# A seventh place for the next expert's first weight unit, copied into the ring by GpSimd

## Chip, cores and metric

One core of a Trainium2 chip runs the whole program. The metric is the device time of one execution in microseconds; the number given for a kernel is the median of its runs.

## What is computed

One layer of a decoder for 256 prompt tokens and 8 x 8 sample tokens, D = 1024, all in float32: modulated RMSNorm, differential attention with a paged cache beside an mLSTM branch, their merge, and then a mixture of experts, which is what the change is about:

```python
logits = (xt @ p['w_router']) + p['b_router']
topv, topi = lax.top_k(logits, TOP_K)             # 4 of 32 experts for each of 320 tokens
...
gu = xb @ p['w_gu'][e] + p['b_gu'][e]             # 1024 -> 2 x 1024
gate = jnp.minimum(gu[:, :D_FF], SWIGLU_LIMIT)
up = jnp.clip(gu[:, D_FF:], -SWIGLU_LIMIT, SWIGLU_LIMIT)
act = (up + 1.0) * gate * jax.nn.sigmoid(SWIGLU_ALPHA * gate)
return (act @ p['w_down'][e] + p['b_down'][e]) * w[:, None]   # 1024 -> 1024, summed over the 4
```

An expert's weights are 12 MB, so the 32 experts read 384 MB; the four gate/up units of an expert hold a quarter of the input rows each, the two down units half of them each.

## The kernel before

The kernel has one hand-written instruction stream for each engine, tied together by semaphores. Everything up to the router is straight-line code. The expert stage is a loop over *blocks*: an expert's tokens are taken 32 at a time (SLOTS), and an expert has one to ten blocks, by how many tokens chose it. With this input there are 55 blocks for 32 experts. The tables with the experts' block counts are made on the chip (`ints`, read back with `value_load` after the semaphore `tables`).

All large weights go through `ring`, six places of 2 MB (`[P, 6, 4096]` float32, 16 KB a partition each). `moe_slot[i]` is the place of an expert's unit i: units 0 to 3 are the gate/up quarters, 4 and 5 the down halves. SP issues the loads in that order, for one expert after another (`expert_weights`, L2217 issues): ahead of unit i of expert e it waits until TensorE has read unit i in all blocks before e (`unit_read[i]`, L2209). `unit_landed` tells of a landing.

TensorE's block (`expert_block`, L1015) runs, in this order: the bias rows; quarter 0; the transposes of the previous block's activations (L989); quarter 1; the previous block's down projection with units 4 and 5; the gather of the next block's tokens; quarter 2; half of the previous block's sums (`combine`); quarter 3; transposes of the gathered rows (L967), the other half of the sums, and transposes of the token weights (L1012). Each quarter waits for its unit's landing (`gate_up_quarter`). Unit 0 of an expert is thus free 2 us into its last block, and units 4 and 5 only in the next expert's first block. Nearly all these matmuls are recorded under L513, the helper `mm`.

VectorE makes the selection tiles of the next gather (L1658, needed by `gather`) and the weighted ones (L1664), adds the sums (L1686) and does the clamps and products of the activation. ScalarE copies from PSUM. GpSimd issues loads and stores before the stage, has nothing to do within it, and stores the outputs at the end.

`hT`, the normalized and transposed tokens, is last read by the router's matmuls and the transposes of `h2`, before the stage.

## Time and profile before

| | |
|---|---|
| time, median of 3 runs | 1680.15 us (1673.82 to 1682.11) |
| profiled execution | 1677.65 us, of which the span is 1675.4 us |
| granted TensorE clock, mean | 0.91 of full speed |
| busy: TensorE, VectorE, ScalarE, GpSimd | 86%, 36%, 16%, 4% |
| DMA | 505.69 MB, mean 302 GB/s |
| expert stage | about 613 to 1642 us of the span |

In the profile PE is TensorE's matmuls and PEld its weight loads, DVE is VectorE, ACT ScalarE, POOL GpSimd and SP the engine that only issues. A q behind the name means the engine's sequencer. The span is the time from the first to the last instruction of the profiled execution; the two microseconds beside it lie around the program. In the timeline, an entry in square brackets gives the idle time ahead of an instruction and what ended it: `<-DMA ring<-in_w_gu` is a wait for a gate/up unit to land. In the stretches table, each row has the stretch, its length, the busy time of PE, PEld, DVE, ACT and POOL (with instructions), the granted share of TensorE's clock, the busy share of the DMA engines and GB/s. A row of the list of waits ends in: us in total, times, longest us. In the views by line, a landing is counted from the issue of the load.

### The profile page before, as it was taken

Reading aid. Unit: us, or ns where it says so; the run is one execution under the profiler, and the core shown is the slowest. Engines: PE = TensorE matmul, PEld = TensorE weight load, DVE = VectorE, ACT = ScalarE, POOL = GpSimd, SP = SyncE. Lnnn points to the kernel's source line nnn. Section 1 sums busy time; section 2 is a strip of 40 time slices with the busy share of each in tenths; the row PEclk is TensorE's granted clock in tenths of the full one; section 3 lists DMA queues with packets and bytes.
Section 4 is the critical chain, followed back from the end, with each engine's and each line's share of the span. In section 5 each row is a group of like instructions: output and inputs, shape, how many; then the busy total and the mean of one; then the engine's idle time right before and its main releaser. Section 6 shows DMA issues by size and latency. Waiting matters only on the chain.

```text
span 1675.4 us, 40558 instructions
## 1 busy us (share of the span) xinstructions
PE 1438.3 (86%) x16467; PEld 804.7 (48%) x16468; DVE 595.4 (36%) x1317; ACT 275.1 (16%) x641; POOL 61.4 (4%) x114
## 2 busy tenths in 40 slices
PE   5798899989999789997999797977959877798794
PEld 3345665557766445553555354533525443344452
DVE  2325553714544333432433233222322423132324
ACT  2004441321210121111111011100101111010111
POOL 2002220000010000000000000000000000000000
PEclk9799998978999979998999899987969988798997
DMA  9525896670057229969999999999999969997850
GB/s 332 193 77 182 294 381 248 211 253 1 1 151 302 101 111 404 388 258 419 404 396 383 424 417 409 426 418 424 401 419 417 408 285 388 417 401 297 369 232 32
DMA packets 80702, 505.69 MB, mean 302 GB/s; under 512 B 6575, under 2 KB 6695, under 8 KB 47666
## 3 DMA queue, kind: packets, MB, share of 16 engines
q1 hardware_dynamic: 72642, 479.86, 71.2%
q0 software_dynamic: 8016, 25.24, 4.6%
q8 instruction: 27, 0.44, 0.1%
q14 instruction: 17, 0.14, 0.0%
HBM read 499.97 MB, written 5.11 MB: 301 GB/s over the span
## 4 chain that ended last, share of the span: by engine, by line
PE 69%; DMA 20%; DVE 6%; issue 2%; ACT 1%; SPq 1%; DVEq 0%; POOL 0%; ACTq 0%; POOLq 0%
PE psum L513 62%; DMA ring<-in_w_gu 15%; DMA ring<-in_w_down 4%; PE psum L672 2%; PE psum L1012 1%; PE psum L967 1%; PE psum L989 1%; DMA ring<-in_w_ada 1%; DVE region L1285 1%; SPq L2217 1%; PE psum L704 0%; ACT region L1773 0%; DVE hT L1171 0%; DVE region L1252 0%; SPq L2222 0%
## 5 line engine op out<-in xcount | busy, mean ns | idle before, releaser
L513 PE MATMUL psum<-ring,region 128*32 128x256 f32 (+1 forms) x11072 | 665.0, 390 | 122.3 <-DMA ring<-in_w_gu 120.2
L513 PEld LDWEIGHTS psum<-ring,region 128*32 128x32 f32 x11072 | 347.6, 114 | 393.7 <-DMA ring<-in_w_gu 131.1
L1686 DVE TENSOR_TENSOR region<-region,psum 128x1280 f32<-128x1280 f32 x110 | 163.2, 1483 | 568.2 <-PE psum L513 568.2
L1773 ACT ACTIVATE region<-psum 128x256 f32<-128x256 f32 (+6 forms) x391 | 164.3, 422 | 1148.8 <-PE psum L513 503.8
L513 PE MATMUL psum<-region 32*128 32x320 f32 (+10 forms) x2652 | 247.2, 421 | 9.4 <-ACT region L1773 3.4
L513 PEld LDWEIGHTS psum<-region 128*32 128x32 f32 (+5 forms) x2652 | 106.3, 139 | 111.2 <-issue 74.5
L513 PE MATMUL psum<-hT,ring 128*128 128x320 f32 x448 | 124.5, 436 | 0.0
L513 PEld LDWEIGHTS psum<-hT,ring 128*128 128x128 f32 x448 | 84.5, 191 | 35.4 <-issue 1.9
L513 PE MATMUL psum<-ring,hT 128*128 128x512 f32 (+1 forms) x192 | 86.4, 607 | 6.1 <-DVE hT L1177 6.1
L1664 DVE TENSOR_SCALAR region<-region 128x128 f32<-128x128 f32 x165 | 47.3, 343 | 98.5 <-issue 98.5
L513 PEld LDWEIGHTS psum<-ring,hT 128*128 128x128 f32 (+1 forms) x192 | 33.1, 177 | 55.0 <-issue 48.7
L672 PE MATMUL psum<-keep,ring 128*128 128x128 f32 x256 | 40.3, 294 | 8.7 <-ACT region L1773 4.4
L513 PE MATMUL psum<-region,ring 128*128 128x320 f32 (+1 forms) x192 | 45.7, 386 | 1.4 <-DVE region L1545 1.4
L2165 POOL DMA_DIRECT2D out_y_prompt<-region x2 | 1.1, 536 | 1126.2 <-DVE region L1764 1126.2
L513 PEld LDWEIGHTS psum<-region,ring 128*128 128x128 f32 x192 | 33.5, 201 | 12.9 <-issue 2.8
L513 PE MATMUL psum<-oT,bias_hot 96*32 96x256 bf16 x440 | 22.1, 276 | 18.8 <-issue 17.5
L672 PEld LDWEIGHTS psum<-keep,ring 128*128 128x128 f32 x256 | 28.9, 147 | 18.7 <-DVE region L1285 10.1
L498 POOL DMA_DIRECT2D ring<-in_cache_v x64 | 34.4, 537 | 76.3 <-issue 76.3
L513 PE MATMUL psum<-region,keep 128*128 128x320 f32 (+7 forms) x90 | 31.5, 481 | 5.2 <-ACT region L2009 3.3
L513 PE MATMUL psum<-ring,cT 128*32 128x512 f32 x192 | 29.7, 768 | 6.8 <-DMA ring<-in_w_ada 6.8
L1012 PE MATMUL psum<-keep,region 128*128 128x128 f32 x165 | 35.2, 291 | 0.0
L1703 DVE TENSOR_SCALAR region<-psum 128x256 f32<-128x256 f32 x55 | 23.3, 424 | 32.4 <-PE psum L513 32.4
(301 smaller groups left out, 886.3 us busy)
## 6 DMA issues: line engine op xcount, KB each, us to landing
ring<-in_w_gu SPq DMA_DIRECT2D x128, 2048.0 KB, 12.2
ring<-in_w_down SPq DMA_DIRECT2D x64, 2048.0 KB, 10.9
ring<-in_w_ada SPq DMA_DIRECT2D x12, 2048.0 KB, 14.5
ring<-in_w_in SPq DMA_DIRECT2D x11, 2048.0 KB, 19.9
ring<-in_cache_k SPq DMA_DIRECT2D x64, 256.0 KB, 5.4
ring<-in_cache_v POOLq DMA_DIRECT2D x64, 256.0 KB, 5.5
ring<-in_w_out SPq DMA_DIRECT2D x2, 2048.0 KB, 22.0
ring<-in_w_up_a SPq DMA_DIRECT2D x1, 2048.0 KB, 10.7
```

Of the source, the lines that this page charges most:

```text
L498: engine.dma_start(dst[:, g, :], cache[bass.ds(page, 1), :, :].rearrange("o p c -> p (o c)"))\
L513: return pe.matmul(out, lhsT, rhs, start=start, stop=stop, skip_group_check=True)
L672: last = pe.transpose(out[:, P * h:P * h + P], kc[:, g, P * h:P * h + P], ident)
L967: last = pe.transpose(psum[:, B_HG, P * j:P * j + P], rows[:, j, :], ident)
L989: last = pe.transpose(psum[:, B_Y, P * j:P * j + P], rows[:, j, :], ident)
L1012: last = pe.transpose(psum[:, B_Y, t0:t0 + m], selw[0:m, j, :], ident[0:m, 0:m])
L1285: dve.tensor_copy(kTb[:, :, PAGE * g:PAGE * g + PAGE], bank("kTb", b, g).rearrange("p (h k) -> p h k", h=H))\
L1664: last = dve.tensor_scalar(selw[:, j, :], lanes, pos[:, j, column], wts[:, j, expert], ALU.is_equal, ALU.mult)
L1686: dve.tensor_tensor(acc_pairs[:, r], acc_pairs[:, r], psum[:, B_SUM:B_SUM + GROUPS, 0:NT], ALU.add)\
L1703: dve.tensor_scalar(act_g, psum[:, B_GATE, 0:WIDE], LIMIT, None, ALU.min).then_inc(gate_clamped, 1)
L1773: return act.activation(out, src, ACT.Copy)
L2217: sp.dma_start(dst, src).then_inc(unit_landed[moe_slot[i]], 16)
```

## The change

The kernel gets one more place of 2 MB, `landing`. It costs no memory: `hT` becomes the tail of `region`, and `landing` covers it and the 1536 columns ahead of it, which held squares that are no longer needed by then. Unit 0 of experts 1 to 31 is loaded there and not into the ring. SP issues that load (`fill_landing`) right behind unit 5 of the expert before, after a wait until that expert's own unit 0 has left the place; the one for expert 1 goes out when the transposes of `h2` are done. GpSimd, in a loop of its own, waits until the ring's place is free and the landing place filled, and copies 128x4096 float32 over in four pieces, each of which raises `first_moved`. TensorE's quarter 0 waits for four pieces in place of the landing. For expert 0, whose unit 0 is loaded as before, four memsets of one word raise the semaphore. SP's loop ends one expert earlier, and the last expert is issued behind it.

```diff
--- before.py
+++ after.py
@@ -135,7 +135,6 @@
 
         ring = sb("ring", [P, RING, UNIT])
         xT = sb("xT", [P, KT, NT])
-        hT = sb("hT", [P, KT, NT])
         keep = sb("keep", [P, n_keep])
         vecT = sb("vecT", [P, 128])
         bias_hot = sb("bias_hot", [P, SLOTS], BF16)
@@ -146,7 +145,8 @@
         small = sb("small", [P, 64])
         oT = sb("oT", [P, H, NT])
         hmT = sb("hmT", [P, H, NT])
-        region = sb("region", [P, REGION])
+        region = sb("region", [P, REGION + KT * NT])
+        hT = region[:, REGION:REGION + KT * NT].rearrange("p (k t) -> p k t", k=KT)
         ints = sb("ints", [1, N_INTS], I32)
         psum = ctx.enter_context(nc.psum_tensor("psum", [P, 8, 512], F32))
 
@@ -288,6 +288,7 @@
         fin_rstd = E.take(3)
         fin_gain = E.take(D)
         x1_sq = Area(REGION - KT * NT).take(KT, NT)
+        landing = region[:, REGION + KT * NT - UNIT:REGION + KT * NT]
         assert E.at <= REGION - KT * NT
         pos = E.take(3, ROUNDS * NE)
         y_out = h2_tok
@@ -302,6 +303,7 @@
         LAM, NLAM, COEF, GS = small[:, 0:4], small[:, 4:5], small[:, 5:6], small[:, 6:7]
         MX, LS, RC = small[:, 8:12], small[:, 12:16], small[:, 16:20]
         M0 = small[0:H, 20:29]
+        pool_word = small[0:1, 40:44]
         BG = small[0:H, 29:31]
         SC = small[:, 32:40]
 
@@ -368,6 +370,8 @@
         blocks_ready = sem("blocks_ready")
         begun_ready = sem("begun_ready")
         bias_in = sem("bias_in")
+        landing_filled = sem("landing_filled")
+        first_moved = sem("first_moved")
         tables = sem("tables")
         mean_inverse = sem("mean_inverse")
         mean_root = sem("mean_root")
@@ -974,7 +978,10 @@
 
             def gate_up_quarter(c, expert):
 
-                pe.wait_ge(unit_landed[moe_slot[c]], 16 * expert + (landed_base[c] + 16))
+                if c == 0:
+                    pe.wait_ge(first_moved, 4 * expert + 4)
+                else:
+                    pe.wait_ge(unit_landed[moe_slot[c]], 16 * expert + (landed_base[c] + 16))
                 u = ring[:, moe_slot[c], :].rearrange("p (j f) -> p j f", j=2)
                 for j in range(2):
                     for q, out_bank in ((0, B_GATE), (1, B_UP)):
@@ -2158,6 +2165,22 @@
             pool.dma_start(bd_rows[0:NE, :], I["b_down"]).then_inc(moe_in, 16)
             pool.dma_start(fin_gain, I["g_final"].to_broadcast([P, D])).then_inc(gain_in, 16)
 
+            first_unit = ring[:, moe_slot[0], :]
+            pool.wait_ge(unit_landed[moe_slot[0]], landed_base[0] + 16)
+            for piece in range(4):
+                pool.memset(pool_word[:, piece:piece + 1], 0.0).then_inc(first_moved, 1)
+            pool.wait_ge(tables, 1)
+            with pool.Fori(1, NE) as e:
+                before = pool.value_load(ints[0:1, bass.ds(e + (AT_BLOCKS - 1), 1)], min_val=1,
+                                         max_val=MAX_BLOCKS)
+                pool.wait_ge(unit_read[0], before)
+                filled = nc.snap(16 * e, [mybir.EngineType.Pool])
+                pool.wait_ge(unit_landed[moe_slot[0]], landed_base[0] + 16)
+                pool.wait_ge(landing_filled, filled)
+                for piece in range(4):
+                    part = slice(UNIT // 4 * piece, UNIT // 4 * piece + UNIT // 4)
+                    pool.tensor_copy(first_unit[:, part], landing[:, part]).then_inc(first_moved, 1)
+
             for j, (t0, n) in enumerate(TILES):
                 for half in range(2):
                     pool.wait_ge(*drained("y", j, half))
@@ -2200,10 +2223,16 @@
             gu = I["w_gu"].rearrange("e (c p j) f -> e c p (j f)", c=4, j=2)
             dn = I["w_down"].rearrange("e (h c p j) f -> e h p c (j f)", h=2, c=2, j=2)
 
+            def fill_landing(expert):
+
+                sp.dma_start(landing, gu[expert, 0].rearrange("o p f -> p (o f)")).then_inc(landing_filled, 16)
+
             def expert_weights(expert, blocks_before):
                 for i in range(RING):
                     if blocks_before is None:
                         sp.wait_ge(*last_use[units[len(units) - RING + i][0]])
+                    elif i == 0:
+                        continue
                     else:
 
                         sp.wait_ge(unit_read[i], blocks_before)
@@ -2217,11 +2246,17 @@
                     sp.dma_start(dst, src).then_inc(unit_landed[moe_slot[i]], 16)
 
             expert_weights(slice(0, 1), None)
+            sp.wait_ge(*full("h2", 2, 1))
+            fill_landing(slice(1, 2))
             sp.wait_ge(tables, 1)
-            with sp.Fori(1, NE) as e:
+            with sp.Fori(1, NE - 1) as e:
                 before = sp.value_load(ints[0:1, bass.ds(e + (AT_BLOCKS - 1), 1)], min_val=1,
                                        max_val=MAX_BLOCKS)
                 expert_weights(bass.ds(e, 1), before)
+                sp.wait_ge(first_moved, 4 * e + 4)
+                fill_landing(bass.ds(e + 1, 1))
+            expert_weights(slice(NE - 1, NE), sp.value_load(
+                ints[0:1, AT_BLOCKS + NE - 2:AT_BLOCKS + NE - 1], min_val=1, max_val=MAX_BLOCKS))
 
 
 _OUTS = [
```

## Rows read from the trace of the kernel before

**Rows 1.** page, part 4: chain that ended last, by engine; first the span
```profile
span 1675.4 us, 40558 instructions
...
PE 69%; DMA 20%; DVE 6%; issue 2%; ACT 1%; SPq 1%; DVEq 0%; POOL 0%; ACTq 0%; POOLq 0%
```

**Rows 2.** stretches table of the expert stage, then its list of waits
```profile
613.00:1642.00 1029.00, 888.61 (x13506) 462.01 (x13505) 318.22 (x707) 125.95 (x330) 0.00 (x0) 0.92 0.91 379
...
PE psum L513 <- DMA ring<-in_w_gu: 120.2, 32, 10.8
```

**Rows 3.** timeline of TensorE, one block: start us, us, what, xcount, [idle before]
```profile
644.67 0.40 PE L513 MATMUL psum<-oT,bias_hot 96*32 96x256 bf16 x8 [0.43 <-issue]
...
644.88 1.92 PE L513 MATMUL psum<-ring,region 128*32 128x256 f32 x32
...
647.16 5.39 PE L513 MATMUL psum<-ring,region 128*32 128x256 f32 x96
...
660.59 0.40 PE L513 MATMUL psum<-oT,bias_hot 96*32 96x256 bf16 x8 [0.37 <-issue]
```

**Rows 4.** timeline of TensorE, a stalled block
```profile
764.12 3.64 PE L513 MATMUL psum<-ring,region 128*32 128x256 f32 x32 [7.61 <-DMA ring<-in_w_gu]
769.02 7.18 PE L513 MATMUL psum<-ring,region 128*32 128x256 f32 x96 [0.63 <-DMA ring<-in_w_gu]
```

**Rows 5.** timeline of TensorE, from three other stalled blocks
```profile
957.20 5.39 PE L513 MATMUL psum<-ring,region 128*32 128x256 f32 x96 [0.62 <-DMA ring<-in_w_gu]
...
966.99 1.93 PE L513 MATMUL psum<-ring,region 128*32 128x256 f32 x32 [0.35 <-DMA ring<-in_w_gu]
...
1351.82 5.39 PE L513 MATMUL psum<-ring,region 128*32 128x256 f32 x96 [1.25 <-DMA ring<-in_w_gu]
...
1590.87 3.64 PE L513 MATMUL psum<-ring,region 128*32 128x256 f32 x32 [7.49 <-DMA ring<-in_w_gu]
```

**Rows 6.** timeline, expert 1, first block; then the chain (start us, us)
```profile
624.78 1.93 PE L513 MATMUL psum<-ring,region 128*32 128x256 f32 x32 [0.30 <-DMA ring<-in_w_gu]
...
629.68 6.88 PE L513 MATMUL psum<-ring,region 128*32 128x256 f32 x96 [2.54 <-DMA ring<-in_w_gu]
...
617.55 12.09 DMA ring<-in_w_gu
```

**Rows 7.** stretches table, the block of rows 4
```profile
756.12:784.24 28.12, 19.52 (x249) 9.10 (x249) 5.86 (x15) 2.26 (x7) 0.00 (x0) 0.76 1.01 428
```

**Rows 8.** timeline of SP's queue: issues of the weight units
```profile
746.53 2.10 SPq L2217 DMA_DIRECT2D ring<-in_w_down  x2
749.76 4.74 SPq L2217 DMA_DIRECT2D ring<-in_w_gu  x4
```

**Rows 9.** issues at 726.6 and 728.9, 746.5, 1235.5, 1327.2, 1432.2 us: to landing
```profile
DMA to landing us min/median/max: 7.4/8.7/10.1
...
DMA to landing us min/median/max: 7.7/7.7/7.7
...
DMA to landing us min/median/max: 9.0/9.0/9.0
...
DMA to landing us min/median/max: 9.8/9.8/9.8
...
DMA to landing us min/median/max: 10.8/10.8/10.8
```

**Rows 10.** VectorE by shape: xcount | busy us, mean ns | idle before
```profile
L1686 DVE TENSOR_TENSOR region<-region,psum 128x1280 f32<-128x1280 f32 x108 | 160.2, 1483 | 561.8 <-PE psum L513 561.8
...
L1658 DVE TENSOR_SCALAR region<-region 128x32 f32<-128x32 f32 x162 | 28.4, 235 | 0.0
L1710 DVE TENSOR_TENSOR region<-region 128x256 f32<-128x256 f32 x55 | 23.4, 425 | 17.2 <-ACT region L2060 17.2
```

**Rows 11.** timeline of VectorE in the block of rows 3
```profile
647.75 0.86 DVE L1664 TENSOR_SCALAR region<-region 128x128 f32<-128x128 f32 x3 [1.73 <-issue]
648.52 0.53 DVE L1658 TENSOR_SCALAR region<-region 128x32 f32<-128x32 f32 x3
```

## The prediction

> **What bounds the kernel now.** I read the page first. The chain that ended last is 69% TensorE and 20% DMA, so neither alone is the bound [rows 1]. The stretches table then puts the expert stage at 1029 of 1675.4 us, with the DMA engines 0.91 busy and TensorE granted 0.92 of its clock; the list of waits says that TensorE stood 120.2 us for gate/up weights, in 32 waits [rows 2]. That is the most an earlier weight unit could give back.
>
> The timeline shows where those waits lie. There are 55 blocks. A block that waits for nothing takes 15.9 us, from 644.67 to 660.59: biases, quarter 0 at 644.88, quarter 1 and the block before's down projection (5.39 us) from 647.16, the gather at about 652.5, quarters 2 and 3 [rows 3]. An expert's six units arrive 4.9 us apart when the queue is full, 29 us together. So an expert of two or three blocks leaves time to load the next, an expert of one block (13 of 32, by the release times) does not, and the expert behind it waits. In all but the first of those cases it looks like this: quarter 0 waits 7.6 us and starts as its unit lands, at 764.12; quarter 1 starts at 769.02, as the second unit lands, 4.9 us later [rows 4]. Twelve blocks have this form, in the last one quarter 0 starts at 1590.87 [rows 5]. Two details matter. Quarter 0 takes 3.64 us there against 1.93 us elsewhere: the granted clock of that stretch is 0.76, so part of it, this quarter included, ran at the lower level of 1.2 GHz after the idle wait [rows 3, 4, 5, 7]. And the idle time ahead of quarter 1 is then 0.63 us, no more [rows 4]. The second unit, not the first, holds the block, but by 0.6 to 1.25 us only [rows 4, 5]; I take 0.7.
>
> **What the seventh place gains.** It lets the next expert's first unit be asked for as soon as the present expert's six are, not when the ring's first unit was read for the last time. But behind a one-block expert that was already so: its two down units were issued at 746.53, and the next expert's first unit followed at 749.76, held by SP's own order [rows 8]. Its landing was 14.3 us after issue, all of it queueing behind the down units. There the new place changes nothing: the transfer waits for the same bytes, 12 times in 12.
>
> Behind an expert of several blocks the first unit does come earlier, and no one waits for it there. What it leaves is a queue shorter by one unit (4.9 us) in that expert's last block. The next five units still wait for TensorE's reads. Where DMA had been idle, an issue lands after 7.4 to 7.7 us; the first down unit of the ten one-block experts that follow a longer one took 7.7 to 9.8 us [rows 9], and only what is above 7.7 can be won, 0 to 2.1 us each, 11 us if all of it goes. What took that excess is not plain (some of it appears with the earlier unit just landing, which the change does not remove), so I take 5 us, bounds 0 and 11. One gain is surer: expert 1. Its first unit now loads in the idle queue before the stage, so its second, issued at 617.55, no longer queues: 7.4 us instead of 12.1, landing at 625.0. Quarter 1 then follows quarter 0 and the transposes, at about 627 instead of 629.68 [rows 6, 9]: 2.5 us.
>
> **What the copy costs.** Each of experts 1 to 31 adds four GpSimd copies of 128x1024 float32, and TensorE's wait for all four before quarter 0. The trace has no copy on GpSimd, so I bound it by VectorE: 425 ns for 256 columns and 1483 ns for 1280 [rows 10] are 1.03 ns a column and 0.16 us fixed, so 1.22 us a piece, 4.9 us for four, and 0.1 us to see the semaphore: **5.0 us**. The low end is half of that, 2.5 us, and the high end twice, 9.9 us; nothing in the trace puts it nearer either, so I take the VectorE figure. The Trainium skill pulls both ways here: "GPSIMD Engine Reference", 4.1 Engine selection, calls one-input elementwise work on this engine roughly line-rate, while "Trainium Architecture — The Big Picture", The five engines, in one table, has streaming elementwise work two times slower than on VectorE. No run shown so far decides between them; by the first page the sum would be the forecast's, by the second that of the slow-copy rival.
>
> Behind a longer expert the copy is hidden: the ring's first unit is read 2.2 us into the last block, the copy ends at 7.3, and quarter 0 of the next block comes at 16.1 [rows 3]. If the copy took over 13 us that cover would be gone. In the twelve stalled blocks it is bare. The landed unit is what TensorE waits for, so quarter 0 starts 5.0 us later; it and the transposes take 4.3 us at the lower clock, and quarter 1, which had 0.7 us to spare, starts 5.0 - 0.7 = 4.3 us late. Everything behind it in the block is TensorE's own work, and the block ends 4.3 us late. Six of the twelve have quarter 3 waiting 0.35 us for its unit as well, as at 966.99, which takes 0.35 us off each [rows 5].
>
> Does the delay last? The next transfers are released by TensorE's reads, so the schedule behind moves with it. Only where the expert is again a single block does the queue have some slack: its first down unit took 9.0 us at 1235.5 and 10.8 us at 1432.2, against 7.7 us unqueued [rows 9], so 1.3 and 3.1 us of those two delays are absorbed before the next wait.
>
> The other edits cost nothing that I can see. The fill's new wait on the copies stands in SP's queue behind the sixth unit's issue, ahead of the next expert's second unit; TensorE needed those copies for quarter 0 of the same block, so it is over long before. The fill for expert 1 waits for the transposes of h2, when SP has nothing else to issue. GpSimd is idle from its last load to the final stores, so its loop, its register load and its four small memsets delay nobody. Folding hT into the region moves addresses and no instruction.
>
> **The sum.** 12 x 4.3 = 51.6; less 6 x 0.35 = 2.1; less 1.3 + 3.1 = 4.4; less 2.5 for expert 1; less 5 for the shorter queue: **+37.6 us**. The profiled execution took 1677.65 us, of which the span is 1675.4, so 1715 for its like. It lies 2.5 us under the median of the runs (1680.15), which makes the forecast 1717.8, said as 1718 us; the times below are on the median's footing too.
>
> With the copy at 2.5 us the delay is 1.8 us: 21.6 - 2.1 - 3.1 - 7.5 = +8.9, or 1689. At 7 us, 6.3 each: 75.6 - 14.0 = +61.6, or 1742. At 9.9 us, 9.2 each: 110.4 - 14.0 = +96.4, or 1777.
>
> **The rivals.** (a) *The copy is slow*, near twice VectorE's time. For it speaks that the trace's GpSimd does nothing but issue DMAs, so nothing vouches for its rate. 1742 to 1777 us. (b) *VectorE and GpSimd get in each other's way.* In a longer expert's last block the copy stands from 2.3 to 7.3 us, as worked out above. VectorE's selection tiles are made from 3.1 to 4.4 us into a block, and the gather needs them at 7.9 [rows 3, 11]. If they had to wait for the last piece they would be ready at 7.3 + 1.3 = 8.6, 0.7 us late, in 18 experts: +13 on top, 1731. Against it: there are gaps between four pieces. The Trainium skill, "SBUF — State Buffer", Who interferes with whom, states such a lock: a port pair shared by the two, held for a whole instruction, which `tensor_scalar` can ask for in its fast mode. (c) *A fast copy*, 2.5 to 4 us: 1689 to 1707. (d) *The other side, faster:* the copy is so short that quarter 0 still ends before the second unit lands. That needs 0.7 us in all or less, 0.2 us a piece, shorter than a 128x32 operation of VectorE (235 ns [rows 10]); then only the gains are left, 2.5 + 11 = 13.5 us, 1667 us. It turns from gain to loss at a copy of about 1.8 us, if all 11 us come. (e) *The place doesn't do what it says*: the fill is never earlier where the stage stalls. That is already in the sum; with the 5 us gone as well it gives 1723.
>
> **How the numbers follow.** Forecast, a copy of 4 to 6 us without (b): 0.50 (with (e) in it). (a) 0.20, (b) 0.10, (c) 0.13, a copy of 1 to 2.5 us, which is no change that could be told: 0.05, (d) 0.02. About 0.5%, 8.4 us, is what a measurement of this kernel can tell from no change. Faster 0.02, same 0.05, slower 0.93. The range 1692 to 1765 leaves out the lower end of (c) and what is under it, and the upper end of (a), some 0.2 together.
>
> **What would show it.** In the new profile: four GpSimd copies of about 1.2 us for each expert, 124 in all; in the twelve stalled blocks a TensorE idle time of 12.5 to 16 us ahead of quarter 0, released by GpSimd and no longer by the DMA, and none ahead of quarter 1; unstalled blocks still at 15.9 us; quarter 1 of expert 1 near 627. Blocks of 16.6 us with the gather waiting for VectorE would mean (b). The forecast is wrong if the copy's time is another (12 us of result for each 1 us of copy), if quarter 0 runs at the full clock behind the longer wait (1.7 us less for each stall), or if the stalls themselves come earlier, which would mean that the fill overtakes something that I hold to be in its way.

## The result, and the profile after

| | before | after |
|---|---|---|
| time, median of 16 runs each | 1679.29 us | 1691.84 us (1682.42 to 1699.36) |
| ratio | 1 | 1.0098, 95% interval 1.0076 to 1.012 |
| profiled execution | 1677.65 us | 1692.39 us |
| span | 1675.4 us | 1690.8 us |
| first block's biases to the last block's | 613.5 to 1625.4: 1011.9 us | 612.7 to 1641.0: 1028.4 us |

The change makes the kernel 1.0% slower, 16 us by the ratio; the two medians stand 12.6 us apart. The forecast had the direction, and put the loss at 38 us. The measured time lies just under the range of 1692 to 1765.

The page of the changed kernel (span, the chain by engine, and GpSimd's group), which answers to rows 1:

```profile
span 1690.8 us, 41005 instructions
...
PE 74%; DMA 13%; DVE 6%; issue 3%; POOL 2%; ACT 1%; SPq 0%; POOLq 0%; DVEq 0%; ACTq 0%
...
L2182 POOL COPY ring<-region 128x1024 f32<-128x1024 f32 x124 | 123.7, 1041 | 943.8 <-DMA region<-in_w_gu 760.0
```

GpSimd copies 124 times, at 1041 ns a piece. Of the 31 groups of four, 27 were released by the landing of the unit and 4 by TensorE's last read of the ring's place. The chain has less DMA (13% for 20%) and more TensorE. The stretches table and the list of waits for the expert stage, against rows 2:

```profile
613.00:1658.00 1045.00, 874.89 (x13501) 459.23 (x13493) 326.32 (x707) 126.07 (x330) 123.68 (x124) 0.92 0.91 371
...
PE psum L517 <- POOL ring L2182: 148.9, 12, 14.4
```

The 120.2 us for gate/up weights are gone, and 148.9 us for GpSimd's copy stand in their place. It is 12 waits and not 32, as every stalled block now waits once only, ahead of quarter 0. The stalled block of rows 4 and the unstalled one behind it, in the timeline of all engines:

```profile
750.72 0.40 PE L517 MATMUL psum<-oT,bias_hot 96*32 96x256 bf16 x8 [0.38 <-issue]
...
758.70 3.99 POOL L2182 COPY ring<-region 128x1024 f32<-128x1024 f32 x4 [33.34 <-DMA region<-in_w_gu]
...
762.74 3.64 PE L517 MATMUL psum<-ring,region 128*32 128x256 f32 x32 [11.62 <-POOL ring L2182]
...
766.94 6.12 PE L517 MATMUL psum<-ring,region 128*32 128x256 f32 x96
...
781.10 0.40 PE L517 MATMUL psum<-oT,bias_hot 96*32 96x256 bf16 x8 [0.37 <-issue]
...
789.60 3.99 POOL L2182 COPY ring<-region 128x1024 f32<-128x1024 f32 x4 [26.91 <-DMA region<-in_w_gu]
...
797.02 0.40 PE L517 MATMUL psum<-oT,bias_hot 96*32 96x256 bf16 x8 [0.37 <-issue]
```

The first unit lands, and GpSimd starts at 758.70. Quarter 0 starts at 762.74, which is 4.04 us behind the start of the copy and 4.17 us behind the landing; in the kernel before it started 0.04 us behind the landing. It ran without pause into quarter 1, which came 4.20 us behind it, where rows 4 have 4.90 us with a pause of 0.63. Quarter 1 and the down projection together took less time than in rows 4 (6.12 us for 7.18). The unstalled block takes 15.92 us as before, and the copy in it is released by the landing, 8.5 us into the block; I had put it at 2.3. Another of the twelve, the first block of rows 5:

```profile
952.35 3.64 PE L517 MATMUL psum<-ring,region 128*32 128x256 f32 x32 [11.62 <-POOL ring L2182]
...
956.42 5.39 PE L517 MATMUL psum<-ring,region 128*32 128x256 f32 x96
```

Expert 1, against rows 6 (the first row is the start of the stage):

```profile
612.66 0.40 PE L517 MATMUL psum<-oT,bias_hot 96*32 96x256 bf16 x8 [0.47 <-ACT region L1780]
...
623.41 1.92 PE L517 MATMUL psum<-ring,region 128*32 128x256 f32 x32
...
625.69 5.39 PE L517 MATMUL psum<-ring,region 128*32 128x256 f32 x96
...
639.22 0.40 PE L517 MATMUL psum<-oT,bias_hot 96*32 96x256 bf16 x8 [0.31 <-issue]
```

Quarter 1 starts at 625.69 for 629.68, and the block takes 16.0 us for 20.6. SP's queue behind the one-block expert of rows 8, and the landing of that fill:

```profile
741.14 2.11 SPq L2246 DMA_DIRECT2D ring<-in_w_down  x2
743.53 0.42 SPq L2228 DMA_DIRECT2D region<-in_w_gu  x1
...
DMA to landing us min/median/max: 15.0/15.0/15.0
```

The fill comes out 2.4 us behind the first down unit, where rows 8 have 3.2, and lands 15.0 us later for 14.3: no gain in the stalls, as forecast. VectorE's two operations that GpSimd could have stood in the way of (rows 10 have the second at 235 ns, and the first took 343 ns before):

```profile
L1671 DVE TENSOR_SCALAR region<-region 128x128 f32<-128x128 f32 x162 | 51.2, 373 | 93.7 <-issue 93.7
L1665 DVE TENSOR_SCALAR region<-region 128x32 f32<-128x32 f32 x162 | 30.9, 250 | 0.0
```

As means they are 30 and 15 ns longer, 7.3 us of busy time over the whole stage. The mean hides what happens: nearly all take as long as before, and in three blocks, where the copy starts 2.5 us into the block, they go in step with its pieces. Rows 11 have 0.86 and 0.53 us for the same two groups:

```profile
721.37 3.99 POOL L2182 COPY ring<-region 128x1024 f32<-128x1024 f32 x4 [36.08 <-PE psum L517]
...
721.99 2.47 DVE L1671 TENSOR_SCALAR region<-region 128x128 f32<-128x128 f32 x3 [1.70 <-issue]
724.37 1.31 DVE L1665 TENSOR_SCALAR region<-region 128x32 f32<-128x32 f32 x3
```

That is what rival (b) describes. The tiles are ready 6.8 us into the block, and the gather starts at 7.7, so these blocks are no longer (15.9 us), and no unstalled block is.

### The profile page after: what moved, and what is told of

Same layout as the page of the kernel before. It is cut to its first block, busy times and chain, and to the rows that moved or that the text cites. A ratio compares the mean times of both kernels' runs of the same rounds, so it can differ in the third digit from the quotient of the medians.

```text
span 1690.8 us, 41005 instructions
## 1 busy us (share of the span) xinstructions
PE 1421.1 (84%) x16467; PEld 800.1 (47%) x16468; DVE 603.2 (36%) x1317; ACT 275.5 (16%) x641; POOL 185.3 (11%) x243
## 4 chain that ended last, share of the span: by engine, by line
PE 74%; DMA 13%; DVE 6%; issue 3%; POOL 2%; ACT 1%; SPq 0%; POOLq 0%; DVEq 0%; ACTq 0%
PE psum L517 67%; DMA region<-in_w_gu 11%; POOL ring L2182 2%; PE psum L676 2%; PE psum L996 1%; PE psum L1019 1%; PE psum L971 1%; DMA ring<-in_w_ada 1%; DVE region L1292 1%; DMA ring<-in_w_gu 1%; PE psum L708 0%; ACT region L1780 0%; DVE region L1178 0%; DVE region L1259 0%; SPq L2246 0%
## 5 line engine op out<-in xcount | busy, mean ns | idle before, releaser
L517 PE MATMUL psum<-ring,region 128*32 128x256 f32 (+2 forms) x11264 | 740.0, 390 | 156.5 <-POOL ring L2182 148.9
L517 PEld LDWEIGHTS psum<-ring,region 128*32 128x32 f32 (+1 forms) x11264 | 378.2, 113 | 465.8 <-POOL ring L2182 152.2
L517 PE MATMUL psum<-region 128*32 128x256 f32 (+11 forms) x2700 | 258.4, 423 | 18.3 <-DVE region L1184 9.0
L2182 POOL COPY ring<-region 128x1024 f32<-128x1024 f32 x124 | 123.7, 1041 | 943.8 <-DMA region<-in_w_gu 760.0
L517 PE MATMUL psum<-region,ring 128*128 128x320 f32 (+1 forms) x640 | 170.1, 421 | 1.4 <-DVE region L1552 1.4
L517 PEld LDWEIGHTS psum<-region,ring 128*128 128x128 f32 x640 | 117.9, 194 | 48.4 <-issue 4.9
L1671 DVE TENSOR_SCALAR region<-region 128x128 f32<-128x128 f32 x165 | 52.1, 373 | 98.5 <-issue 98.5
L1019 PEld LDWEIGHTS psum<-keep,region 128*128 128x128 f32 x165 | 18.5, 139 | 32.9 <-issue 32.9
L1665 DVE TENSOR_SCALAR region<-region 128x32 f32<-128x32 f32 x168 | 31.9, 250 | 0.0
L996 PEld LDWEIGHTS psum<-keep,region 128*128 128x128 f32 x110 | 17.2, 206 | 26.9 <-issue 25.7
L1717 DVE TENSOR_TENSOR region<-region 128x256 f32<-128x256 f32 x55 | 23.4, 426 | 17.0 <-ACT region L2067 16.8
## 6 DMA issues: line engine op xcount, KB each, us to landing
region<-in_w_gu SPq DMA_DIRECT2D x31, 2048.0 KB, 15.5
ring<-in_w_out SPq DMA_DIRECT2D x2, 2048.0 KB, 20.6
```

The costliest lines, as they stand in the source:

```text
L517: return pe.matmul(out, lhsT, rhs, start=start, stop=stop, skip_group_check=True)
L996: last = pe.transpose(psum[:, B_Y, P * j:P * j + P], rows[:, j, :], ident)
L1019: last = pe.transpose(psum[:, B_Y, t0:t0 + m], selw[0:m, j, :], ident[0:m, 0:m])
L1665: last = dve.tensor_scalar(sel[:, j, :], lanes[:, 0:SLOTS], pos[:, j, column], None, ALU.is_equal)
L1671: last = dve.tensor_scalar(selw[:, j, :], lanes, pos[:, j, column], wts[:, j, expert], ALU.is_equal, ALU.mult)
L1717: dve.tensor_tensor(act_g, act_g, act_s, ALU.mult).then_inc(gs_ready, 1)
```

## The sum, term by term

The same times can be read in each of the twelve stalled blocks of both profiles: from the block's start to the landing, from there to quarter 0, from there to quarter 1, from there to the next block's start, and the block after. Their sums over the twelve, after less before:

| term | forecast | measured |
|---|---|---|
| landing to quarter 0, for the copy, 12 times | 60.0 (5.0 us) | 49.5 (4.17 us for 0.04) |
| quarter 0 to quarter 1 | -8.4 | -10.6 |
| quarter 1 to the block's end | -2.1 | -9.3 |
| landing of the first unit, from the block's start | -9.4 (queue 5.0, slack 4.4) | -6.8 |
| expert 1 | -2.5 | -4.6 |
| other blocks (five took 16.2 to 16.3 us before) | 0 | -1.8 |
| sum | +37.6 | +16.4 |

Two things carry the difference of 21 us: the copy held quarter 0 for 0.9 us less each time (10.5), and the blocks were quicker from quarter 0 on by more than I had counted (2.2 to quarter 1, 7.2 behind it). The second is a matter of the clock. Six of the twelve quarters 0 rose to full speed within the quarter and took 3.23 to 3.62 us for 3.64; in three blocks of the kernel before this happened too, but quarter 1 then waited for its own unit and could not follow sooner. The stretches table for the first three parts of rows 4's stalled block in the kernel before (stretch, length, busy PE, PEld, DVE, ACT, POOL, granted clock, DMA share, GB/s):

```profile
764.12:769.02 4.90, 4.27 (x34) 1.71 (x35) 0.00 (x0) 0.38 (x1) 0.00 (x0) 0.50 1.00 428
769.02:772.70 3.68, 3.68 (x36) 1.77 (x40) 0.00 (x0) 0.00 (x0) 0.00 (x0) 0.50 1.00 427
772.70:776.00 3.30, 3.30 (x64) 1.80 (x60) 0.00 (x0) 0.00 (x0) 0.00 (x0) 1.00 1.05 447
```

and the like in the changed kernel:

```profile
762.74:766.94 4.20, 4.20 (x35) 1.69 (x35) 0.00 (x0) 0.00 (x0) 0.00 (x0) 0.50 0.99 421
766.94:768.30 1.36, 1.36 (x17) 0.66 (x20) 0.00 (x0) 0.38 (x1) 0.00 (x0) 0.50 1.02 434
768.30:773.00 4.70, 4.70 (x92) 2.63 (x88) 0.00 (x0) 0.00 (x0) 0.00 (x0) 0.98 0.95 373
```

In both TensorE had been idle for 8 to 12 us, and restarts at 0.50 of the clock, its 1.2 GHz level. Before, it pauses 0.63 us ahead of 769.02 and stays there for 8.6 us in all. After, it does not pause and is at full speed about 5.7 us behind quarter 0's start. Before, five of the other stalled blocks did the same, while six were back at full speed by quarter 1: 13.4 us from quarter 1 to the block's end, against 15.2 to 15.5. After, all twelve lie between 13.4 and 14.3. The quick ones end at 13.4 us with the wait of 0.35 us ahead of quarter 3 (before) and without it (after), so the 2.1 us forecast for these waits came to nothing, and all of the 9.3 us are the clock's.

## The experiments

All ratios are against runs of the kernel before on the same chip in the same session. "Stage" is the time from the first block's biases to the last's.

| run | ratio to before (95%) | stage, us | quarter 1 to block's end, twelve blocks |
|---|---|---|---|
| before | 1 | 1011.9 | six at 13.4, six at 15.2 to 15.5 |
| e5_before_again | one run, 1666 us | 1009.2 | seven at 13.4, five at 15.2 to 15.6 |
| after | 1.0098 (1.0076 to 1.012) | 1028.4 | 13.4 to 14.3 |
| e8_after_again | 1.0099 (1.0077 to 1.012) | 1027.9 | 13.4 to 14.1 |
| e1_no_copy | 0.9889 (0.9849 to 0.993) | 999.0 | 13.4 to 14.1 |
| e2_piece_waits | 0.9926 (0.9904 to 0.9948) | 1005.3 | 13.4 to 14.1 |
| e3_late_fill | 1.0118 (1.0084 to 1.0152) | 1031.4 | 13.4 to 13.9 |
| e4_copy_twice | 1.048 (1.0438 to 1.0521) | 1086.3 | 13.4 to 14.2 |
| e6_no_pause | 1.0244 (1.0219 to 1.0269) | 1051.7 | 13.4 to 14.1 |
| e7_half_us_delay | 0.995 (0.993 to 0.9971) | 1003.5 | 13.4 to 14.2 |
| e9_pause_filled | 1.0006 (0.9981 to 1.0031) | 1012.6 | 13.4 to 14.0 |
| e10_one_copy | one run, 1687 us | 1028.6 | 13.4 to 14.1 |

### e1_no_copy: the seventh place with a copy of no cost

```diff
-                    pool.tensor_copy(first_unit[:, part], landing[:, part]).then_inc(first_moved, 1)
+                    pool.memset(pool_word[:, piece:piece + 1], 0.0).then_inc(first_moved, 1)
```

> GpSimd's four copies are replaced by four memsets of one word, so nothing moves from the landing place into the ring (TensorE reads the ring's old unit 0 for every expert: that part of the result is left out). What is left is the seventh place with a copy of no cost. My theory: the copy is the whole of the loss, and the early place itself gives a little: 4.6 us at expert 1 and some us from a shorter queue, so 5 to 14 us faster than the kernel before, 1665 to 1674. Rival 1: the seventh place itself costs (the extra wait in SP's queue, the transfers in another order): at or above the kernel before, 1679 or more. Rival 2: the seventh place is worth as much as was meant, a 4.9 us unit for each of 13 stalls: about 50 us faster, 1630.

The kernel leaves out the move of the data, and so part of the result. 1657.87 us, 0.9889 of the kernel before: 18.6 us faster, 12 to 25 by the interval; 5 to 14 had been expected. Rivals 1 and 2 fall. Taken with the changed kernel's 1.0098 the copy costs 2.1%, 35 us. The timeline of the second of the stalled blocks:

```profile
943.59 3.60 PE L517 MATMUL psum<-ring,region 128*32 128x256 f32 x32 [9.12 <-POOL small L2182]
...
948.17 5.39 PE L517 MATMUL psum<-ring,region 128*32 128x256 f32 x96 [0.54 <-DMA ring<-in_w_gu]
```

The memsets still delay quarter 0 by 0.3 us. All twelve blocks are quick from quarter 1 on. In the stage's 12.9 us less than before, 10.6 come from there; that part is no merit of the seventh place, as e7 will show.

### e4_copy_twice: the copy doubled

```diff
+                copied = nc.snap(4 * e, [mybir.EngineType.Pool])
                 for piece in range(4):
                     part = slice(UNIT // 4 * piece, UNIT // 4 * piece + UNIT // 4)
+                    pool.tensor_copy(first_unit[:, part], landing[:, part]).then_inc(copied_once, 1)
+                pool.memset(pool_word[:, 0:1], 0.0)
+                pool.wait_ge(unit_landed[moe_slot[0]], landed_base[0] + 16)
+                pool.wait_ge(copied_once, copied)
+                for piece in range(4):
+                    part = slice(UNIT // 4 * piece, UNIT // 4 * piece + UNIT // 4)
                     pool.tensor_copy(first_unit[:, part], landing[:, part]).then_inc(first_moved, 1)
```

> The changed kernel with the four copies made twice over, the second time after a wait for the first; only the second time tells TensorE. A copy of 4.0 us becomes one of about 8.2. My theory: a stalled block pays all of it, 12 x 4.2 = 50 us, less 3 to 7 us that the queue's slack absorbs behind one-block experts: 43 to 48 us above the changed kernel, 1735 to 1740. Rival (the loss is from the wait's place or from VectorE standing behind GpSimd in the other blocks): other than in proportion to the stalls; with VectorE behind it, unstalled blocks longer than 15.9 us and over 60 us in all.

1.048 of the kernel before, 3.8% or 64 us above the changed kernel, and 58 us in the stage: more than the 43 to 48 us expected. The twelve stalled blocks pay 41.7 us of it ahead of quarter 0: the second copy holds it 4.1 us longer, 49.5 us in all, less 7.8 us as the units land earlier from the block's start. That is in proportion to the stalls. The rest, 16 us, is in other blocks, nearly all of it in three that did not stall before. GpSimd's and then TensorE's timeline, a block whose expert follows one of two blocks:

```profile
651.14 3.99 POOL L2184 COPY ring<-region 128x1024 f32<-128x1024 f32 x4 [26.82 <-DMA region<-in_w_gu]
...
655.26 4.40 POOL L2190 COPY ring<-region 128x1024 f32<-128x1024 f32 x4
...
656.12 0.40 PE L518 MATMUL psum<-oT,bias_hot 96*32 96x256 bf16 x8 [0.36 <-issue]
659.72 3.43 PE L518 MATMUL psum<-ring,region 128*32 128x256 f32 x32 [3.19 <-POOL ring L2190]
```

The fill had landed at 651.1, 18 us behind its issue, and not early in the last block; 8.5 us of copies reach 3.3 us past the point where quarter 0 wants them. So the cover that I gave the copy ("over 13 us") was 5.2 us here, and 7.6 us in the unstalled block of the changed kernel above. The changed kernel's 4.0 us fit in it; a copy of 9.9 us would not have.

### e3_late_fill: the early place made useless

```diff
-            fill_landing(slice(1, 2))
             sp.wait_ge(tables, 1)
+            sp.wait_ge(unit_read[0], sp.value_load(ints[0:1, AT_BLOCKS:AT_BLOCKS + 1], min_val=1,
+                                                   max_val=MAX_BLOCKS))
+            fill_landing(slice(1, 2))
...
                 sp.wait_ge(first_moved, 4 * e + 4)
+                after_this = sp.value_load(ints[0:1, bass.ds(e + AT_BLOCKS, 1)], min_val=1,
+                                           max_val=MAX_BLOCKS)
+                sp.wait_ge(unit_read[0], after_this)
                 fill_landing(bass.ds(e + 1, 1))
```

> The changed kernel, but the landing place is filled no earlier than the ring's first place was before: SP waits for TensorE's last read of unit 0 ahead of each fill, for expert 1 too. The copy is as it was. It is the changed kernel with its seventh place made useless. My theory: expert 1's gain of 4.6 us is lost and the 4 to 6 us from the shorter queue, so 8 to 11 us above the changed kernel, 1700 to 1703. Rival (the early place is worth nothing): 1692. Rival (it is worth what was meant): far above, 1740.

1.0118, against 1.0098 and 1.0099 for the changed kernel: 3 us above, and the intervals overlap. 8 to 11 us had been expected. The trace says where the difference lies. Expert 1's first block:

```profile
620.95 0.40 PE L517 MATMUL psum<-oT,bias_hot 96*32 96x256 bf16 x8 [0.76 <-DVE bias_hot L1677]
626.14 3.64 PE L517 MATMUL psum<-ring,region 128*32 128x256 f32 x32 [4.79 <-POOL ring L2182]
...
630.15 5.39 PE L517 MATMUL psum<-ring,region 128*32 128x256 f32 x96
...
643.67 0.40 PE L517 MATMUL psum<-oT,bias_hot 96*32 96x256 bf16 x8 [0.46 <-issue]
```

It takes 22.7 us for 16.0: 6.7 us lost, since the copy is now bare there too. The rest of the stage is 3.6 us shorter than in the changed kernel, and not longer. So in these profiles the early place is worth something at expert 1 alone. The 5 us that I gave the shorter queue are not seen.

### e2_piece_waits: TensorE waits piece by piece

```diff
-                if c == 0:
-                    pe.wait_ge(first_moved, 4 * expert + 4)
-                else:
+                if c:
                     pe.wait_ge(unit_landed[moe_slot[c]], 16 * expert + (landed_base[c] + 16))
...
                     for q, out_bank in ((0, B_GATE), (1, B_UP)):
+                        if c == 0:
+                            pe.wait_ge(first_moved, 4 * expert + (2 * j + q + 1))
```

> The changed kernel, but TensorE's quarter 0 waits for one piece ahead of each fourth of its matmuls (a piece of 1024 columns is just what one fourth reads) and not for all four ahead of the first. Copies of 1.0 us and fourths of 0.9 us (at the lower clock) then overlap, and quarter 1 comes 0.7 us late in a stalled block and no longer 3.1 us. My theory: 12 x 2.4 = 29 us less than the changed kernel's 1692, or 1663; if the short waits between the fourths keep the granted clock low for longer, up to 9 us of that are lost: 1672. Either way faster than the kernel before (1679). Rival (it is not the bare copy that costs, but what lies around it): unchanged, 1692.

1662.78 us, 0.9926 of the kernel before (0.9904 to 0.9948): the lowest ratio of the versions with all of the work in them, though e7's interval overlaps it, and faster than the kernel before and the changed one. GpSimd's copies and then TensorE, in the second of the stalled blocks:

```profile
939.16 4.00 POOL L2182 COPY ring<-region 128x1024 f32<-128x1024 f32 x4 [28.65 <-DMA region<-in_w_gu]
...
940.26 4.04 PE L517 MATMUL psum<-ring,region 128*32 128x256 f32 x32 [9.53 <-POOL ring L2182]
...
944.86 6.03 PE L517 MATMUL psum<-ring,region 128*32 128x256 f32 x96
```

Quarter 0 starts 1.1 us behind the start of the copy for 4.04, takes 4.0 us for 3.6 beside the copies, and quarter 1 follows without pause, 5.8 us behind the landing, where the kernel before has 4.9. The theory holds: the edit takes away the bare copy and with it the loss. The expected 1663 us stood on the footing of the result's runs; there 0.9926 is 1667 us, between the 1663 and the 1672 for a clock held low by the short waits. Against the kernel before, e2 has no sooner quarter 1 in a stalled block. What it wins is 4.7 us at expert 1 (15.9 us for 20.6) and 8.7 us behind quarter 1, the clock effect that the next runs take apart.

### e5_before_again, e7_half_us_delay, e6_no_pause: is it the pause?

That the kernel before was slow in half of its stalled blocks could be chance. A second profile of it:

> The kernel before, profiled once more. In its first profile six of the twelve stalled blocks ran quarter 1 and the down projection partly at the lower clock (the block ended 15.1 to 15.5 us behind the start of quarter 1), the other six did not (13.4 us). Theory A (the 0.6 us pause between quarter 0 and quarter 1 keeps the clock low): again about half of the twelve are slow, of whichever experts. Theory B (it is chance in one execution): all or none may be slow; with none, the 9 us that the change seemed to win here are no effect of it.

Five of twelve, four of them the same as in the first profile's six and one other. The like row to rows 4:

```profile
755.66 3.64 PE L513 MATMUL psum<-ring,region 128*32 128x256 f32 x32 [7.40 <-DMA ring<-in_w_gu]
...
760.56 7.43 PE L513 MATMUL psum<-ring,region 128*32 128x256 f32 x96 [0.63 <-DMA ring<-in_w_gu]
```

Then the kernel before with quarter 0 a little late, so that the pause goes and quarter 1 hardly moves:

```diff
+            with pool.Fori(1, NE) as e:
+                seen = nc.snap(16 * e + (landed_base[0] + 16), [mybir.EngineType.Pool])
+                pool.wait_ge(unit_landed[moe_slot[0]], landed_base[0] + 16)
+                pool.wait_ge(unit_landed[moe_slot[0]], seen)
+                for piece in range(8):
+                    word = pool.memset(pool_word[:, piece:piece + 1], 0.0)
+                    if piece >= 4:
+                        word.then_inc(first_seen, 1)
...
-                pe.wait_ge(unit_landed[moe_slot[c]], 16 * expert + (landed_base[c] + 16))
+                if c == 0:
+                    pe.wait_ge(first_seen, 4 * expert + 4)
+                else:
+                    pe.wait_ge(unit_landed[moe_slot[c]], 16 * expert + (landed_base[c] + 16))
```

> The kernel before, but TensorE learns of the first unit's landing through GpSimd, which waits for it and runs eight memsets of one word (0.1 us each), the last four of which tell TensorE. Quarter 0 of a stalled block starts 0.7 to 0.8 us late, the pause ahead of quarter 1 is gone, and quarter 1 starts 0.1 us late at most. Nothing else changes, no seventh place. Theory A (the pause keeps the clock low): all twelve blocks end 13.4 to 14.2 us behind quarter 1, some 8 us faster than the kernel before, 1666 to 1671. Theory B (chance): equal to the kernel before or 1 to 2 us slower.

0.995 (0.993 to 0.9971): a kernel with a delay added to each stall is 8 us faster, as theory A has it. None of the twelve is slow. A stalled block of it, GpSimd and then TensorE:

```profile
1040.46 0.37 POOL L2174 MEMSET small<- 1x1 f32 x8 [29.15 <-DMA ring<-in_w_gu]
...
1040.88 3.64 PE L515 MATMUL psum<-ring,region 128*32 128x256 f32 x32 [9.03 <-POOL small L2174]
...
1045.29 6.15 PE L515 MATMUL psum<-ring,region 128*32 128x256 f32 x96
...
1059.47 0.40 PE L515 MATMUL psum<-oT,bias_hot 96*32 96x256 bf16 x8 [0.36 <-issue]
```

The delay was 0.5 us, not the 0.7 to 0.8 expected (eight memsets take 0.37 us together), and a pause of 0.13 us was left; it did no harm. Next, the kernel before with a full delay and no copy:

```diff
+                if c == 0:
+                    pe.wait_ge(unit_landed[moe_slot[1]], 16 * expert + (landed_base[1] + 16))
                 pe.wait_ge(unit_landed[moe_slot[c]], 16 * expert + (landed_base[c] + 16))
```

> The kernel before, but quarter 0 waits for the second unit's landing too: in a stalled block both quarters start 4.9 us after the first unit landed, with no pause between them and no copy anywhere. It is a delay of quarter 1 by 4.3 us at the lower clock (3.6 us of quarter 0 and 0.7 of transposes), against 3.1 us in the changed kernel. Theory A (no pause, so the clock is back by quarter 1): the blocks end 13.4 to 14.2 us behind quarter 1, and the whole is 12 x 4.3 - 4.5 (queue's slack) - 9 (clock) = 38 us above the kernel before, 1712 to 1717. Theory B: half of them still slow, 47 us above, 1721 to 1726.

1714.9 us, 1.0244, 41 us above: between the two theories' numbers, but the twelve blocks all lie between 13.4 and 14.1, as A alone has it. It also prices a bare delay without GpSimd or a seventh place. Quarter 0 comes 5.0 us later behind its landing, 59.6 us in the twelve blocks; the units land 6.2 us earlier, quarter 1 follows 10.2 us sooner and the blocks end 8.0 us sooner, much as in the sum above (6.8, 10.6, 9.3), and 4.6 us are lost at expert 1 and in other blocks. So the changed kernel's loss needs no other cause than the delay. The changed kernel again beside them:

> The changed kernel once more, on the same chip as the others: 1.0% above the kernel before, with its stalled blocks ending 13.4 to 14.2 us behind quarter 1 (theory A), or half of them at 15.2 us (theory B).

1.0099, the same as the first time, and no slow block.

### e9_pause_filled: the pause filled, the start unmoved

e7 also moves the start of quarter 0, and that could be what helped (theory C). This run does not move it:

```diff
-                for j in range(2):
-                    last = pe.transpose(psum[:, B_Y, P * j:P * j + P], rows[:, j, :], ident)
+                for again in range(2):
+                    for j in range(2):
+                        last = pe.transpose(psum[:, B_Y, P * j:P * j + P], rows[:, j, :], ident)
                 last.then_inc(act_turned, 1)
```

> The kernel before, with the two transposes between quarter 0 and quarter 1 made twice in every block (the second time gives the same values). Quarter 0 starts with its landing as before; in a stalled block the 0.62 us pause ahead of quarter 1 is filled with TensorE work, in the other 43 blocks the extra pair costs 0.43 us. Theory A (it is the pause that keeps the clock low, not the moment at which quarter 0 starts): all twelve stalled blocks end 13.4 to 14.2 us behind quarter 1, 7 to 11 us won, 43 x 0.43 = 18 us lost, +7 to +11 us or 1.005 of the kernel before. Theory C (it is the later start of quarter 0 that helped in the half-microsecond run): five or six of the twelve still at 15.1 to 15.6 us, +18 us or 1.011.

```profile
1046.14 3.64 PE L513 MATMUL psum<-ring,region 128*32 128x256 f32 x32 [8.28 <-DMA ring<-in_w_gu]
...
1051.03 5.66 PE L513 MATMUL psum<-ring,region 128*32 128x256 f32 x96 [0.19 <-DMA ring<-in_w_gu]
```

Quarter 0 starts with its landing and quarter 1 with its own, 4.89 us apart as before; the pause is 0.19 us. All twelve are quick (13.4 to 14.0). Theory C falls, on one profile, of another chip than e5 to e8. The whole is 1.0006, since the extra pair costs 0.23 us a block (16.15 us for 15.92) and not 0.43: 10 us lost, as much won.

### e10_one_copy: fixed cost and rate

```diff
-                for piece in range(4):
-                    part = slice(UNIT // 4 * piece, UNIT // 4 * piece + UNIT // 4)
-                    pool.tensor_copy(first_unit[:, part], landing[:, part]).then_inc(first_moved, 1)
+                pool.tensor_copy(first_unit, landing).then_inc(first_moved, 4)
```

> The changed kernel with one GpSimd copy of 4096 columns in place of four of 1024. It parts the copy's fixed cost from its rate. If the 0.16 us fixed cost of VectorE held here as well, four pieces of 1.0 us are 0.84 us of columns each, and one copy takes 3.5 us; the run is then 12 x 0.5 = 6 us below the changed kernel. If the pieces overlap in their fixed part, it takes 4.0 us as before and nothing moves.

```profile
L2180 POOL COPY ring<-region 128x4096 f32<-128x4096 f32 x31 | 111.6, 3601 | 951.1 <-DMA region<-in_w_gu 771.5 <-PE psum L517 179.5
```

3601 ns for 4096 columns and 1041 for 1024 give 0.83 ns a column and 0.19 us fixed. The four pieces overlap by 0.05 us each. Quarter 0 starts 0.36 us sooner behind its landing, 4.3 us in the twelve blocks, but the stage is no shorter (1028.6 for 1028.4): the first units landed 4.0 us later from their blocks' starts, which a single profile can't tell from chance. GpSimd and VectorE in a block where the copy starts early:

```profile
715.62 3.60 POOL L2180 COPY ring<-region 128x4096 f32<-128x4096 f32 x1 [36.40 <-PE psum L517]
...
716.22 3.59 DVE L1671 TENSOR_SCALAR region<-region 128x128 f32<-128x128 f32 x3 [1.71 <-issue]
```

The first of the three VectorE operations took 3083 ns, up to the end of the copy; in e1, without copies, all of this form are at 343 ns.

## Why the prediction was wrong

**The direction and the main mechanism were right.** The stalls sit behind one-block experts; the fill comes no earlier there; GpSimd's copy is bare in twelve blocks, and hidden in the others. e1 shows that without the copy the loss is gone, e3 that the early place is worth nothing in those twelve, and e6 that a bare delay is paid for by the same terms in a kernel without the copy.

**The size was wrong in two terms.** First, *the copy's time*: "1.03 ns a column and 0.16 us fixed", taken from VectorE, against 0.83 and 0.19 (e10). Landing to quarter 0 grew by 4.13 us and not 5.0, times twelve: 10.5 of the 21 us. The step that failed is the choice between the bounds 2.5 and 9.9 us by VectorE's rows; that these came within about a fifth was luck. They were not even the nearest rows: both are operations with two inputs, and the same trace has copies of VectorE with one input, from on-chip memory to on-chip memory (SBUF), as GpSimd's are:

```profile
L1422 DVE COPY region<-region 128x192 f32<-128x192 f32 x1 | 0.3, 263 | 0.0
L1421 DVE COPY region<-region 128x24 f32<-128x24 f32 x1 | 0.2, 181 | 0.0
```

These two, one operation each, give 0.49 ns a column, so an estimate of 0.67 us for 1024 columns on VectorE; GpSimd's 1041 ns are 1.6 times that. Of the two pages of the Trainium skill, "GPSIMD Engine Reference", 4.1 Engine selection (one input, roughly line-rate) fits if the rate is that of rows 10: 1041 ns is under the 1.22 us worked out from them. The table in "Trainium Architecture — The Big Picture", The five engines, in one table (two times slower than VectorE) is near what the copies within SBUF show. No run has VectorE make this very copy, so neither page is refuted here.

With the copy's true 4.13 us the prediction's own sum gives +27 us, or 1707, inside the range and still well above what was measured. The second term takes 9.4 us more off: *"Everything behind it in the block is TensorE's own work, and the block ends 4.3 us late"*. The block's own work was not a constant. I had seen that quarter 0 ran at the lower level in the stalls, and had the two rows with 7.18 and 5.39 us for the same 96 matmuls before me (rows 4 and 5), without asking what the difference was. It was the 0.6 us pause ahead of quarter 1, which the change removes: with the pause, six (then five) of the twelve blocks stay at the lower level into the down projection, without it none does (e6, e7, e9, and all runs of the changed kernel). At the blocks' ends this gives back 9.3 us, where the forecast had 2.1 for another reason. The 2.2 us more between the quarters are not the pause's: there the clock rose within quarter 0, and nothing held quarter 1.

**Smaller misses.** "I take 5 us" for the shorter queue: e3 shows nothing of it. Expert 1 gained 4.6 us and not 2.5: quarter 1 came 3.1 us sooner from the block's start, and it and the down projection took 5.39 us for 6.88, as the pause of 2.54 us (rows 6) and the clock of 0.54 behind it, from 629.68 to 633.00, are gone. The cover of the hidden copies was put at over 13 us, as I had let the fill land early where it is queued behind five others. It is that only for the 4 of 31 copies that start early, and 5.2 and 7.6 us in the two blocks shown where the copy waits for its landing. Rival (b) was judged too light: VectorE does wait, up to 1.07 us an operation here and 3.08 us in e10. It costs nothing here, as the two meet in three blocks only, not 18, and the gather comes late enough.

**What held:** 124 copies, a wait for GpSimd and none ahead of quarter 1, 15.9 us for unstalled blocks. The idle times ahead of quarter 0 were 11.6 to 14.4 us for the 12.5 to 16 expected. The time falls among those of rival (c) (1689 to 1707), but its reason, a copy of 2.5 to 4 us, is only half of what happened.

**Open.** What decides which of the paused blocks stay at the lower level: 8 of 19 did not. With the clock effect in both, e1 (999.0 us) and e7 (1003.5 us) differ by 4.5 us of stage; 3.2 of it is expert 1's block (16.0 for 19.2), and the last 1.3 us are within what landings vary. A true seventh place, read where it lies, was not tried. e1 does not price it: of its 12.9 us of stage, 10.6 come from the clock, by way of the 0.3 us that its memsets delay quarter 0, and a place read directly would have no such delay.

## What to carry to other kernels

In this kernel a buffer more did not help, as the queue ahead of the stalled transfer was already full; look at the issue time of the late transfer, and not at the wait. A copy between a landing and its reader is on the critical path exactly where the wait is, and it should be waited for in the pieces in which it is read: that one edit turned +1.0% into -0.7%. It does not make the place pay, though: e7, which has no seventh place, has 0.995 and a stage 1.8 us shorter than e2's. Where TensorE restarts at the lower clock after a long wait, a second short wait behind it can cost more than its own length, and half a microsecond of delay (e7), or of filler (e9), can pay for itself. And look at single operations, not at their mean, when two engines may stand in each other's way.

## What the runs showed of the hardware

**A pause of 0.6 us behind the restart.** In two profiles of the kernel before, 24 stalled blocks, 19 ran quarter 0 wholly at the 1.2 GHz level and then paused 0.6 us, and 11 of these stayed at that level until 8.4 to 9.4 us behind quarter 0's start. In the ten profiles of kernels in which a block still at the lower level pauses 0 to 0.3 us, none of 120 did, though 65 of them were still at the lower level 4.15 us behind quarter 0's start; the latest was back at full speed 6.1 us behind quarter 0's start. "TensorE: Matmul & The Clock Gate" of the Trainium skill, A second HAM failure mode: psum-queue depth-cycling, tells of a kernel whose short idle times between groups of matmuls keep the clock moving between its levels. These runs show something near it but not the same: one short pause, and a rise that comes later (8.4 us and more for 6.1 at most), with no fall in between.

**GpSimd copies float32 within SBUF at 0.83 ns a column** (e10). VectorE's two-input operations of rows 10 take 1.03, its own copies within SBUF 0.49 (two rows, above).

**VectorE can wait for a GpSimd copy.** The 128x128 operation that takes 343 ns took 1.07 us beside copies of 1.04 us, and 3.08 us beside one of 3.60 us (e10), in three blocks of either profile; in e1, without copies, none is longer than before.

**A load issued shortly before the one ahead of it lands can be late.** The landings, in the changed kernel, of the first down units issued at 1023.9 and 1416.9 us:

```profile
DMA to landing us min/median/max: 10.4/10.4/10.4
...
DMA to landing us min/median/max: 7.5/7.5/7.5
```

The first was issued 2.9 us before the unit ahead of it landed (1026.8) and came 7.5 us behind it; the second, 1.6 us before (1418.5), came 5.9 us behind, and its 7.5 us from issue are no more than a load takes into an idle queue (rows 9). Over seven traces (before, after, e1, e2, e3, e4, e6), loads issued 5 us or more ahead of the previous landing come 4.8 to 5.6 us behind it, and those issued 1.5 to 4 us ahead anywhere from 4.9 to 8.4. This is the "excess" that the prediction left unexplained, and the early place moves such cases about without removing them. What does it was not tried.
